# VectorE evicts a tile ahead of the low parts of the weights two tiles on, in the projections with features on partitions

## The reference

```
# first block
h = even_layer(h)   # p = rmsnorm(x) @ w_in; q, k by a causal convolution and silu; mLSTM; pooling; out = x + y @ w_out
h = odd_layer(h)    # q, ckv, indexer, z = rmsnorm(x) @ w_in; k, v = ckv @ w_uk, ckv @ w_uv; top 128 keys; out = x + (o * silu(z)) @ w_out
# second block
h = h + swa_sink_mixer(rms_norm(h))       # qkv projection, window of 128, sinks, w_o
h = h + swiglu(rms_norm(h))               # (silu(h @ gate) * (h @ up)) @ w_down, width 2816
h = h + nsa_mixer(rms_norm(h))            # projection, compressed, selected and window attention, w_o
h = h + swiglu(rms_norm(h))
return rms_norm(h, final_norm)
```

## Time and profile before

| | us |
|---|---|
| median of three runs | 2103.03 |
| lowest, highest | 2102.55, 2109.07 |
| the profiled execution | 2101.56 |
| its span, from the first instruction to the last | 2099.8 |
| TensorE busy | 2007.8 (96%) |
| VectorE busy | 1056.8 (50%) |
| ScalarE busy | 785.5 (37%) |
| POOL busy | 271.9 (13%) |

### The profile page before, as it was taken

How to read it: one execution, slowest core, us unless ns; L and a number is a source line. 1 busy time by engine, 2 the same in 40 slices (tenths; PEclk the granted TensorE clock), 3 DMA queues, 4 the chain that set the end, 5 groups by cost and what they waited for, 6 DMA issues and landing times. The chain is left out here.

```text
span 2099.8 us, 25252 instructions
## 1 busy us (share of the span) xinstructions
PE 2007.8 (96%) x9730; PEld 1532.6 (73%) x9730; DVE 1056.8 (50%) x1971; ACT 785.5 (37%) x1389; POOL 271.9 (13%) x376
## 2 busy tenths in 40 slices
PE   6989999999999999989999999999799999999998
PEld 5776777887757557757788888877556678888886
DVE  5556643444578555475544443343466654444322
ACT  3233333433333464364322222224277642223222
POOL 2540000001000231042000000000155310000000
PEclk9999999999999999989999999999699999999999
DMA  7452234443322113212333333345100123333331
GB/s 175 127 160 66 65 110 141 141 141 85 81 71 71 51 32 104 78 41 80 91 91 100 91 95 93 93 112 165 50 2 2 31 86 105 91 95 96 93 91 68
DMA packets 316685, 186.81 MB, mean 89 GB/s; under 512 B 33503, under 2 KB 297183, under 8 KB 316310
## 3 DMA queue, kind: packets, MB, share of 16 engines
q1 hardware_dynamic: 310158, 168.29, 28.4%
q10 hardware_dynamic: 6408, 16.91, 2.1%
HBM read 182.95 MB, written 17.96 MB: 96 GB/s over the span
## 5 line engine op out<-in xcount | busy, mean ns | idle before, releaser
L247 PE MATMUL banks<-xs,wlo 128*128 128x512 f32 x1336 | 539.2, 404 | 5.0 <-PEq L1440 2.8
L1595 DVE TENSOR_TENSOR wlo<-raw,whi 128x1024 fp32r<-128x1024 f32 (+1 forms) x283 | 359.5, 1271 | 350.9 <-ACT whi L1586 350.7
L248 PE MATMUL banks<-xs,whi 128*128 128x512 f32 x1336 | 529.1, 396 | 0.0
L249 PE MATMUL banks<-xs,whi 128*128 128x512 f32 x1336 | 529.1, 396 | 0.0
L1586 ACT ACTIVATE whi<-raw 128x1024 fp32r<-128x1024 f32 (+1 forms) x283 | 293.5, 1038 | 249.5 <-PE banks L249 183.2
L247 PEld LDWEIGHTS banks<-xs,wlo 128*128 128x128 f32 x1336 | 251.6, 188 | 79.3 <-issue 16.6
L248 PEld LDWEIGHTS banks<-xs,whi 128*128 128x128 f32 x1336 | 251.6, 188 | 62.7 <-issue 3.3
L249 PEld LDWEIGHTS banks<-xs,whi 128*128 128x128 f32 x1336 | 251.5, 188 | 60.7
L2097 ACT ACTIVATE prob<-prob,stat 128x384 f32<-128x384 f32 (+5 forms) x256 | 136.5, 534 | 92.9 <-DVE stat L2035 91.0
L409 POOL TENSOR_TENSOR squares<-squares,x_tmp 128x512 f32<-128x512 f32 x35 | 46.9, 1340 | 748.7 <-ACT x_tmp L401 748.7
L247 PE MATMUL banks<-a_hi,wlo 128*128 128x512 f32 x352 | 139.9, 397 | 0.0
(11 more groups left out here) (330 smaller groups left out, 2775.1 us busy)
## 6 DMA issues: line engine op xcount, KB each, us to landing
raw<-in_ffn_w_gu SPq DMA_DIRECT2D x88, 512.0 KB, 3.8
raw<-in_e_w_in SPq DMA_DIRECT2D x56, 512.0 KB, 3.8
raw<-in_ffn_w_down SPq DMA_DIRECT2D x32, 512.0 KB, 4.0
s_skew<-s_bias ACTq DMA_DIRECT2D x6, 2560.0 KB
raw<-in_o_w_in SPq DMA_DIRECT2D x21, 512.0 KB, 4.0
raw<-in_e_w_out SPq DMA_DIRECT2D x16, 512.0 KB, 3.8
raw<-in_b_w_in SPq DMA_DIRECT2D x15, 512.0 KB, 3.8
raw<-in_ffn_w_down SPq DMA_DIRECT2D x16, 384.0 KB, 3.4
```

The source lines that it names most:

```text
L247: nc.tensor.matmul(out, k.wlo[:, chunk.slot, at, :], self.x_hi(kt), start=first, stop=False)
L248: nc.tensor.matmul(out, k.whi[:, chunk.slot, at, :], self.x_lo(kt), start=False, stop=False)
L249: ins = nc.tensor.matmul(out, k.whi[:, chunk.slot, at, :], self.x_hi(kt), start=False, stop=last)
L1595: self.nc.vector.tensor_tensor(self.wlo[:, chunk.slot, 0:chunk.blocks, :], self.raw[:, chunk.slot, 0:chunk.blocks, :], hi.bitcast(F32), AL ...
```

## The change

In `Dense.on_dve` the low part of chunk c + 2 moves from the head of VectorE's list for chunk c to behind the evictions of that chunk. The loop over the tiles that end with the chunk is split in two: one for the row scale and the evictions, one for the work beside. ScalarE's list, TensorE's, POOL's and SP's are as before, and so is `DenseRows`. From here on all lines of the changed kernel have a number that is higher by one.

```diff
     def on_dve(self, dve):
         k = self.k
         for c in range(self.first, self.last):
-            k.split_low(dve, c + AHEAD)
             for n in self.ending(c):
                 if n == 0 and self.scale is not None:
                     self.scale.dve(dve)
                 if n == 0 and self.evicted is not None:
                     self.evicted(dve)
                 self.evict(dve, "dve", n)
+            k.split_low(dve, c + AHEAD)
+            for n in self.ending(c):
                 for b in self.beside:
                     b.dve(dve, n)
```

## The result

| | before | changed |
|---|---|---|
| median, us | 2102.79 (4 executions) | 2121.65 (4 executions) |
| lowest, highest | 2102.41, 2109.07 | 2120.08, 2122.24 |
| span of the profiled execution | 2099.8 | 2119.3 |

The changed kernel is slower: the ratio is 1.008, with a 95% interval from 1.0062 to 1.0097. The direction was forecast. The size was not: the median is 18.9 us above that of before where 12.1 was forecast, and 1.15 above the upper end of the range.

A forecast was written before the change was run, and what follows sets the result against it. TensorE, busy 96% of the span, was taken as the bound, so only its idle time and low clock count. 11.4 - 5.6 + 1.4 + 1.7 + 1.2 + 1.5 + 0.5 = +12.1 gave 2113.6 us, range 2107 to 2120.5.

The forecast's parts named there:

- The third tiles: Third tile of five projections that start with a norm: TensorE waits 1.4 to 3.0 us for the low part, +11.4.
- 200 steady tiles: Steady loops of the gate/up and residual projections: about 1.8 to 2.1 us spare, so no gain or loss.
- first rival: The clock also falls in the four new stalls of 2.8 to 3.7 us: 6.8 more, 2120.4 us; chance 0.15.
- `o_uk`: Four-tile chunk: variance slides behind fourth eviction and subtraction, so ScalarE's square for the third tile is late: +1.5 us.
- fourth rival: Loads go out about a tile later, while bias tables are copied in DRAM: more than 2121 us; chance 0.05.
- `b_rest`: SyncE's loads go out some 5 us later, so a low part just misses TensorE's date: +0.5 us.
- The end of `e_out`: One more subtraction, beside POOL's addition, at the block's end: +1.4 us, idle time 2.82 to 4.2.
- The clock behind that end: TensorE's clock falls after the 4.2 us of idle time between e_out and o_in: +1.7 us, bounds 0 and 1.7.
- `e_qk`: Earlier eviction removes TensorE's 3.92 us wait for ScalarE's silu and the low clock behind it: -5.6 us.
- The end of `o_z`: The last masks come behind the subtraction at the end of o_z: +1.2 us.
- third rival: A wait behind each stall gives the 11.4 us back: 2102.2 us; chance 0.07 together with faster still.

The follow-up runs named there:

- the last kernel: The kernel before, with the low part behind the eviction in e_qk and behind the first of four evictions in o_uk and o_uv: 2096.78 us, ratio 0.9957.

## Why the prediction was right in sign and a third too small

**The third tiles: right.** The five waits were forecast as 11.4 and cost 10.9, of which 9.9 are waits in TensorE's rows and the rest goes at the five restarts, 0.15 to 0.27 each. The two in `ff_gu` are shorter by 0.15, since the subtraction starts 0.08 ahead of the eviction's end (1743.49 against 1743.57) and the hand-over is 0.05. The prediction's way, to set the end of the eviction plus one subtraction against the start of the matmuls, found each of them, and none that isn't there: 200 steady tiles lost nothing.

**The clock behind them: the step that failed, 4.9 us.** The prediction named this as its first rival and priced it at 1.7 a stall (measured 1.61 to 1.65), but gave it 0.15. So its sum took this clock at nothing. The reason was one row: 2.82 us of idle time at the end of `e_out` with a clock of 1.00 behind it. The experiments show that this row is no rule: two of four kernels with that same idle time have 0.79 and 0.64 there. Within the projections the clock fell behind 20 of 22 stalls of 1.9 us or more at a third tile, in seven traces, and behind eight of eight in `o_uk`. The page "TensorE: Matmul & The Clock Gate" of the Trainium skill, section "HAM oscillation — how this bites in real kernels", describes waits of 3 to 5 us between bursts of matmuls that put the array back at half rate. The stalls in question here are shorter, and the runs show the same behind them: the third tile behind 2.49 us is at 0.77, and so is one behind 1.91. The prediction set one row against the rival, and took the row. The rival had a price of 2120.4 and a stretch up to 2121, and the median lies 0.65 above that stretch, where the prediction had only its fourth rival, loads that come too late. The trace has a late load at one place, `b_rest`, and 0.43 us for it. It is the first rival that came true, on top of the two terms below that were too small.

**The end of `e_out`: term too small by 0.8.** The step was "1.2 to 1.5, I take 1.4", from a subtraction of 1.51 beside POOL's addition. The row was read without asking how far the two overlap. Here is that addition, in the kernel before:

```profile
1705.91 1.34 POOL L409 TENSOR_TENSOR squares<-squares,x_tmp 128x512 f32<-128x512 f32 x1 [4.29 <-ACT x_tmp L401]
```

It ends at 1707.25, only 0.43 behind the start of the subtraction at 1706.82. The subtraction lost 0.28 of those 0.43, so it stood still for most of the time that was left of the addition. In the changed kernel the same two in the next instance of that loop:

```profile
1726.68 1.34 POOL L410 TENSOR_TENSOR squares<-squares,x_tmp 128x512 f32<-128x512 f32 x1 [4.27 <-ACT x_tmp L402]
1726.78 2.32 DVE L1596 TENSOR_TENSOR wlo<-raw,whi 128x1024 fp32r<-128x1024 f32 x1
```

The subtraction starts 0.10 behind the addition, and 2.32 is the 1.24 that the addition leaves (1728.02 - 1726.78) plus 1.08. Against 1.23 alone it lost 1.09: in both rows 0.15 less than what was left of the addition. The page "SBUF — State Buffer" of the Trainium skill, section "Who interferes with whom", says that such a pair blocks each other for a whole instruction; the prediction worked out 2.5 by it and went by 1.4, and the trace has 2.24. That none of the other 34 long subtractions stalls TensorE is as the prediction had it: 1.8 us of spare less 1.1.

**The clock behind that end** was forecast as 1.7 and is 1.26, and 2.7 in the second trace of the same kernel (8.58 us for a first tile that takes 5.84 before). In all seven traces with 3.98 to 5.05 us of idle time here the first tile ran at a low clock, in 7.11 to 8.60 us; behind 2.82 us it did so in two of six. That speaks for the longer wait as the cause, as the prediction had it, but does not show it, since two kernels with the old idle time have the loss too.

**`o_uk`: term too small by 2.6.** The mechanism was the forecast one, and the two sizes that were missed make up the whole difference. First, the wait of 1.17 did not go: a subtraction moved ahead of the search step of `o_q`'s last tile, and the eviction came behind both as before. The prediction had started its chain 1.17 earlier for it. With that taken back, its 1.5 is 2.67, and the trace has 3.68 - 1.02 = 2.66; that they agree to 0.01 is luck, since 0.4 of overlaps in that sum were a guess. Second, the clock fell behind the wait, which is the rest, 1.46 (0.86 of it in the two sums of squares, 1.89 against 1.03).

**`e_qk`: right**, -5.87 for -5.6. **The end of `o_z` and `b_rest`: right**, 1.14 and 0.43 for 1.2 and 0.5, the latter with the late load that was forecast. **Nothing was given back**: the third rival has no trace anywhere, as the matmuls behind each stall run on without a wait.

## What to carry to other kernels

Before one moves a step behind another in an engine's list, it pays to look for the few instances where the other is late (the first tile behind a norm, a chunk with several tiles, the last tile of a block): the steady loop hid some 200 instances here, and ten decided. Such a rule is better applied to the places that gain by it than to a whole class: the eviction ahead in `e_qk`, `o_uk` and `o_uv`, with the loop in one piece, is 0.3 to 0.4% faster, in all of them and with the loop split 0.8% slower. A stall of TensorE is to be priced with what the clock does behind it, and a row that speaks against that price is worth as much as the number of its instances in the trace: one was not enough.

## What the runs showed of the hardware

- A stall of TensorE of up to 1.1 us in a stream of matmuls left the granted clock at 1.00 (13 stalls at third tiles, 5.86 or 5.87 us for 24 matmuls). Behind 19 of 21 stalls from 1.91 to 2.71 us at such a tile it took 7.34 to 7.42 us, at a mean clock of 0.77 or 0.78; behind the two others 5.9 at 1.00. Behind 4.67 us it was at 0.50 from the first matmul on.
- At one place, behind 2.81 or 2.82 us between two blocks, the first tile ran at 1.00 in four traces (three of the kernel before, one of the last kernel), and at 0.79 and 0.64 in one each of two others. Behind 3.98 to 5.05 us at that place it was low in seven of seven, 0.65 to 0.80.
- VectorE's subtraction of two tensors in SBUF (128x1024, 1.23 us) and POOL's addition (128x512, 1.31 us) do not run side by side: the subtraction takes 2.3 us where both start together, 1.51 where the addition had 0.43 to go, 1.24 where it is cut to 0.27 us.
